# Sums of squares of q and k by two rounded products instead of one full fp32 product

## The chip, the cores and the metric

One core of a Trainium2 chip runs the whole program in one launch. The metric is the device time of that launch in microseconds (us). The engines are named as the profile names them: PE is TensorE, DVE is VectorE, ACT is ScalarE, POOL is GpSimd, SP is SyncE, whose queue issues the DMAs here.

## The reference

A first block (a gated linear recurrence beside windowed attention) and then two layers of a second block work on 256 tokens of width 2048. The change touches the two layers. There, attention normalises q and k by the mean of their squares over each head of 64, and the delta-rule branch normalises q and k of six heads of 128 by the sum of their squares:

```python
qa = apply_partial_rope(rms_norm_2(qa.reshape(bsz, T, A_Q_HEADS, A_HEAD_DIM), q_norm_w[l]), cos, sin)
ka = apply_partial_rope(rms_norm_2(ka.reshape(bsz, T, A_KV_HEADS, A_HEAD_DIM), k_norm_w[l]), cos, sin)
...
def l2_norm(x):
    return x * lax.rsqrt(jnp.sum(x * x, axis=-1, keepdims=True) + EPS)
...
q = l2_norm(q.reshape(bsz, T, C_HEADS, C_HEAD_DIM))
k = l2_norm(k.reshape(bsz, T, C_HEADS, C_HEAD_DIM))
```

## The kernel before

Activations are kept transposed: a tile has 128 features on the partitions and 256 tokens in the free dimension. The large products read their weights in slots of 1 MB (128x2048). A slot is loaded by SP into `w_raw`, rounded by ACT to the type fp32r into `w_hi` (`Ring.round`, L274), and DVE takes the rest `w_raw - w_hi` into `w_lo` (`Ring.residual`, L282). PE then sums three products of rounded operands (hi by hi, hi by lo, lo by hi) for each row of weights. A slot of features is 48 products of 256 columns (`Ring.features`, L309). The ring has five places, so a load starts when the slot five before it is used up; rounding and rest are done some two to three slots ahead of PE.

A layer has 68 slots. Four kinds of slot matter here:

- slots 8 to 11 make k and v of the attention, slots 12 to 17 its q, two slots for each pair of tiles;
- slots 24 to 41 make q, k and v of the six heads of the delta rule, three slots a head;
- slots 42 to 51 make gates, with the chain of the delta rule placed between their products;
- slots 52 to 67 are the output product.

All order is written out by hand. Each engine has one list of instructions for the layer (`sync`, `scalar`, `vector`, `tensor`, `gpsimd` in `layer_parts`), carried out in that order, and the lists are tied by counting semaphores.

The sums of squares over the partitions are products with a matrix of ones on PE. For the attention, ACT squares a pair of tiles into `q_sq` (128x512, L1700 and L1734) and PE multiplies it by `blocks`, ones within each half of 64 (L2582 for k, L2604 for q in `turn_queries`, in the middle of slots 15, 17 and 19). For head h of the delta rule, ACT squares q and k into `sq` (128x512, L1819, at the end of `silu_qk`) and PE multiplies by `ones` (L2652 in `sum_squares`), in the middle of the slot two after the head's last one, or, for the last head, after slot 43. These operands are full fp32, so each of these products stands as two instructions in the trace. A layer has 10 such sums: one for k, three for q, six for the heads.

During the heads' slots the lists of DVE and ACT are tied to each other. For iteration h, DVE's list is: `norm(h - 2)`, `open_heads(h - 1)` (y_now, L2231), the rest of a slot, the convolution of v of the head before (L2241, three taps), `normalise(h)` (L2222), the convolution of q, the rest of a slot, the convolution of k, `soften(h + 1)` (L2197 and on), the rest of a slot. Between them stand pieces of a convolution of 31 taps (L2086, called taps here), of which the last six instructions stand in iteration 3. ACT's list is: a slot's rounding, the evacuation of v (`head_in`), `round_a` (L1786, waits for y_now), `exps`, a slot's rounding, `silu_qk(h - 1)` with the square, `head_in(h, 0)` (L1799, for which DVE's convolution of q waits), and so on. PE waits for the last taps with the first sum of the branch (L2656, after slot 34) and for `normalise` with `flip` (L2635).

POOL does little in a layer: it clears two buffers, prepares masks, takes rests of the attention's output (`split_a`, L2953, one a head), weighs decays (L2967) and takes the rests of the other branch (`branch_split`, L2957).

Of the kernel before, what the change touches and what calls it, by code (L numbers as in the profile page):

```python
# [9 lines left out]
F32 = mybir.dt.float32  # L10
# [378 lines left out]
def first_parts(k, t, s):  # L389
# [933 lines left out]
    "ylo "  # L1323
    "rounded12 split12 bg zcopied rows_in negexp gexped gchain sums scalars scexps "
    "copied conv silued squared summed std norm "
    "bsummed centred bsquared bsquares bstd bln lsig hid bmixed bsteps byrounded bylo "
    "rows grown prepared masked decays weighted ended gout "
# [40 lines left out]
    "ylo": 6, "weighted": 6, "bylo": 4, "stored": 0,  # L1368
}


# [40 lines left out]
def layer_parts(k, t, s, layer):  # L1412
# [23 lines left out]
    assert goto(units_at) <= units_at, "kept parts"  # L1436
    before_decay, until_decay = put("before_decay", [P, 2, H, CHUNK]), put("until_decay", [P, 2, H, CHUNK])
    grown = [put(f"grown{g}", [P, 4, P]) for g in range(G)]
    state_a, vnew = put("state_a", [P, H, P]), put("vnew", [P, G, P])
    o_first = put("o_first", [P, G, P])  # L1440
    second_at = goto(units_at)

    q_raw = [put(f"q_raw{n}", [P, 2, T]) for n in range(2)]
    q_sq, rstd, part = put("q_sq", [P, 2, T]), put("rstd", [P, 2, T]), put("part", [P, 2, T])
    turn = put("turn", [P, P])
    v_rest = put("v_rest", [P, KT - 2 * V_ROWS, V_STEP])
# [49 lines left out]
    padded = put("padded", [P, 3, PAD + T])  # L1496
    goto(k.y_at + 26 * 4 * T)
    conv, sq = put("conv", [P, 3, T]), put("sq", [P, 2, T])
    goto(k.feat_at)
    qk = put("qk", [P, 2 * H, T])  # L1500
    std, bstd = put("std", [P, 2, T]), put("bstd", [P, T])
# [105 lines left out]
    def sync(sp):  # L1607
        ring.load(sp, 3)
        ring.load(sp, 4)
        if layer == 0:  # L1610
            sp.wait_ge(k.first.oroot, 1)
            sp.wait_ge(k.first.ow, 8)
        sp.dma_start(params[:], k.p2[layer]).then_inc(s.p2_in, 16)
        if layer == 0:
            sp.wait_ge(s.joined, since.joined + 10)
            for m in range(2):
                sp.dma_start(t["state"][:, m], x_in[:, m]).then_inc(k.kept, 16)
        ring.load(sp, 5)
        sp.dma_start(sink_row[:], t["sinks_2"][layer:layer + 1].to_broadcast([P, HEADS_2])).then_inc(s.tables_in, 16)
        ring.load(sp, 6)  # L1620
        sp.dma_start(mask[:], constant(k, "window_2")).then_inc(s.tables_in, 16)
        sp.dma_start(cumulate[:], constant(k, "cumulate")).then_inc(s.tables_in, 16)
        sp.dma_start(before[:], constant(k, "before")).then_inc(s.tables_in, 16)
        sp.dma_start(not_before[:], constant(k, "not_before")).then_inc(s.tables_in, 16)
        ring.load(sp, 7)
        sp.dma_start(levels[:].rearrange("p l t -> p (l t)"), constant(k, "levels")).then_inc(s.tables_in, 16)
        sp.dma_start(level_t[:], constant(k, "level_t")).then_inc(s.tables_in, 16)
        sp.dma_start(ident_c[:], constant(k, "ident_c")).then_inc(s.tables_in, 16)
        sp.dma_start(pw[:].rearrange("p a n -> p (a n)"), k.pw[layer]).then_inc(s.tables_in, 16)
        there, arrived = (t["state"], k.kept) if more else (t["out"], s.stored)  # L1630
        for n in range(8, SLOTS_2 + AHEAD):
            ring.load(sp, n)
            if n == 12:
                sp.wait_ge(s.used, since.used + 8)
                sp.dma_start(turn[:], constant(k, "turn_2")).then_inc(s.narrow_in, 16)
                sp.dma_start(v_rest[:].rearrange("p k n -> p (k n)"), k.v_rest[layer]).then_inc(s.narrow_in, 16)
                sp.dma_start(rows[:].rearrange("p a n -> p (a n)"), k.rows_c[layer:layer + 1].to_broadcast([P, 2 * H]))\
                  .then_inc(s.rows_in, 16)
            if n == SLOT_OUT2 + 4:
                sp.wait_ge(s.used, since.used + SLOT_OUT2)  # L1640
                sp.wait_ge(s.bylo, since.bylo + B)
                sp.wait_ge(k.kept, kept_before)
                sp.dma_start(x_t[:], t["state"]).then_inc(s.xin, 16)
            if n == SLOT_OUT2 + 4 and more:

                sp.dma_start(k.norm_w[:], t["p2"][layer + 1, :, P2_NORM:P2_NORM + KT]).then_inc(s.weight_in, 16)
            if n in (SLOT_OUT2 + 11, SLOT_OUT2 + 13, SLOT_OUT2 + 17):
                c = (SLOT_OUT2 + 11, SLOT_OUT2 + 13, SLOT_OUT2 + 17).index(n)
                for m in range(2):
                    sp.wait_ge(s.added, since.added + 2 * c + m + 1)  # L1650
                    sp.dma_start(there[:, m, cols(c)], x_t[:, m, cols(c)]).then_inc(arrived, 16)
        for m in range(2):
            sp.wait_ge(s.added, since.added + 7 + m)
            sp.dma_start(there[:, m, cols(3)], x_t[:, m, cols(3)]).then_inc(arrived, 16)
        if more:
            sp.wait_ge(s.weight_in, since.weight_in + 16)

    def scalar(act):
# [52 lines left out]
        act.activation(v_rest_hi[:], v_rest[:], ACT.Copy).then_inc(s.rounded12, 1)  # L1711
        key_in(1)
        ring.round(act, SLOT_KV + 6)
        act.wait_ge(s.kturned, since.kturned + 2)
        root(aux[3], rstd[:], s.krstd, since.krstd)
        ring.round(act, SLOT_Q + 3)
        act.wait_ge(s.bg, since.bg + 1)
        for b in range(2):
            act.activation(z12[:, b, 0::2], z[b][:, T:V_COLS:2], ACT.Copy).then_inc(s.zcopied, 1)
# [81 lines left out]
        def silu_qk(h):  # L1801
            if h == 0:
                act.wait_ge(k.kept, kept_before)
            act.wait_ge(s.conv, since.conv + 9 * h + 6)
            if h % 2:
                for e in range(2):
                    for i in range(2):
                        ins = act.activation(swapped(qk[:, 2 * h + i], 1 - e), swapped(conv[:, i], e), ACT.Silu)
                    ins.then_inc(s.silued, 1)
            else:  # L1810
                act.activation(qk[:, 2 * h:2 * h + 2], conv[:, 0:2], ACT.Silu).then_inc(s.silued, 1)
            act.wait_ge(s.conv, since.conv + 9 * h + 9)
            if h % 2:
                for e in range(2):
                    act.activation(swapped(v_all[:, h], 1 - e), swapped(conv[:, 2], e), ACT.Silu).then_inc(s.silued, 1)
            else:
                act.activation(v_all[:, h:h + 1], conv[:, 2:3], ACT.Silu).then_inc(s.silued, 1)
            act.wait_ge(s.silued, since.silued + silus_before(h) + 1 + h % 2)
            act.activation(sq[:], qk[:, 2 * h:2 * h + 2], ACT.Square).then_inc(s.squared, 1)  # L1819

        def root_qk(h):
            act.wait_ge(s.summed, since.summed + h + 1)
# [711 lines left out]
    def tensor(pe):  # L2534
# [28 lines left out]
        for j in range(B):  # L2563
# [4 lines left out]
            if j == 0:  # L2568
                pe.wait_ge(s.whole, since.whole + wholes)
                spread_root(pe, k, s, since, KT - 4 * first_c)  # L2570

        pe.wait_ge(s.opened, since.opened + 3)
        for b in range(2):
            ring.features(pe, SLOT_KV + b, tile(2 + b), k.xn_hi, k.xn_lo, None if b else normed_rows)
# [4 lines left out]
        pe.wait_ge(s.kcopied, since.kcopied + 2)  # L2579
        pe.wait_ge(s.emptied, since.emptied + 2)  # L2580
        pe.matmul(aux[2][:, 0:2 * T], turn[:], q_raw[1][:], start=True, stop=True).then_inc(s.kturned, 1)
        pe.matmul(aux[3][:, 0:2 * T], k.blocks[:], q_sq[:], start=True, stop=True).then_inc(s.kturned, 1)  # L2582
        ring.values_and_gates(pe, SLOT_KV + 3, 1, with_gates, k.xn_hi, k.xn_lo)
        pe.wait_ge(s.split12, since.split12 + 1)
        for kk in range(KT - 2 * V_ROWS):
            row = 2 * V_ROWS + kk
# [6 lines left out]
        def turn_queries(i):  # L2593
# [7 lines left out]
                pe.wait_ge(s.rstd, since.rstd + 2)  # L2601
            at = 2 * (i % 2)
            pe.matmul(aux[at][:, 0:2 * T], turn[:], q_raw[i % 2][:], start=True, stop=True).then_inc(s.qturned, 1)
            pe.matmul(aux[at + 1][:, 0:2 * T], k.blocks[:], q_sq[:], start=True, stop=True).then_inc(s.qturned, 1)  # L2604

        def cumulated():
            pe.wait_ge(s.tables_in, since.tables_in + 144)
# [40 lines left out]
            ins.then_inc(mixed[p], 1)  # L2648

        def sum_squares(h):  # L2650
            pe.wait_ge(s.squared, since.squared + h + 1)
            pe.matmul(z[3][:, 0:2 * T], k.ones[:], sq[:], start=True, stop=True).then_inc(s.summed, 1)  # L2652

        def branch_sum(what):
            for b in range(B):
# [254 lines left out]
        for i, (c, w) in enumerate(OUT_ORDER):  # L2910
# [6 lines left out]
                    pe.wait_ge(s.added, since.added + 2 * (c - 1))  # L2917
            if c == 0 and w:
                if w == 1:
                    pe.wait_ge(s.bylo, since.bylo + B)  # L2920
                else:
                    pe.wait_ge(s.olo, since.olo + 1 if w == 2 else G)
            if i < 15:
# [8 lines left out]
    def gpsimd(pool):  # L2932
# [6 lines left out]
        pool.wait_ge(k.kept, 2 * 16)  # L2939
        pool.wait_ge(s.rowed, since.rowed + 1)  # L2940
        pool.memset(padded[:], 0.0).then_inc(s.cleared, 1)
        pool.wait_ge(s.tables_in, since.tables_in + 144)
        pool.wait_ge(s.scalars, since.scalars + 1)
        for r in range(2):
# [9 lines left out]

        def branch_split(b):
            pool.wait_ge(s.byrounded, since.byrounded + b + 1)
            pool.tensor_tensor(k.y_lo[:, 6 + b], yb_now[:, (b + 2) % B], k.y_hi[:, 6 + b].bitcast(F32), ALU.subtract).then_inc(s.bylo, 1)  # L2957

        for u in range(4):
            split_a(u)  # L2960
        for g in range(G):
            if g < 2:
                split_a(4 + g)
            pool.wait_ge(s.decays, since.decays + 2 * g + 1)
            for r in range(2):
                there = before_decay[:, r, 2 * g:2 * g + 2]
# [197 lines left out]
```

## Time and profile before

| what | value |
| --- | --- |
| median of 3 runs | 1921.54 us (1921.5 to 1923.63) |
| time of the profiled execution | 1921.74 us |
| its span, first to last instruction | 1920.0 us |
| granted TensorE clock over the span | 0.998 |
| PE busy | 1900.8 us (99%) |
| DVE busy | 1276.0 us (66%) |
| ACT busy | 1104.2 us (58%) |
| POOL busy | 70.5 us (4%) |
| DMA | 171 GB/s mean |

The time is the span and 1.74 us around it. Busy time of PE counts overlapping matmuls once; the duration of one matmul in the rows (0.28 us for 256 columns) is its passage through the array, and the next one starts before it ends, so a product's cost is read from the distance between starts.

### The profile page before, as it was taken

The numbers are of one execution on the slowest core, as the hardware profiler recorded it, in microseconds if no ns is written. First come the engines' busy times: TensorE is split into PE (matmuls) and PEld (weight loads), VectorE is DVE, ScalarE is ACT, GpSimd is POOL, SyncE is SP. The second block draws the span as 40 slices with busy tenths as digits, with TensorE's granted clock in tenths as the row PEclk, the third lists the DMA queues.
The fourth block names the chain that finished last, engine by engine and source line by source line (L and its number), as shares of the span: only waits on it lengthen the run. The fifth ranks groups of instructions, "written<-read, shape, count | busy, mean of one in ns | idle before, by whom it ended". The sixth has DMA issues, their size and how long they took to land.

```text
span 1920.0 us, 31625 instructions
## 1 busy us (share of the span) xinstructions
PE 1900.8 (99%) x13516; PEld 1703.3 (89%) x13516; DVE 1276.0 (66%) x1791; ACT 1104.2 (58%) x1506; POOL 70.5 (4%) x66
## 2 busy tenths in 40 slices
PE   9999999999999999999999999999999999999998
PEld 8999988888888888888899999998889999999887
DVE  7778766655544444655699898754658988876453
ACT  7787755554533333434656688926465577893541
POOL 0111100000000000000000000100000000010000
PEclk9999999999999999999999999999999999999999
DMA  7454454444455555565564443322666544432163
GB/s 265 181 185 183 160 189 169 154 154 163 164 197 194 188 191 198 191 247 197 188 230 154 176 141 146 132 76 98 225 215 223 176 156 157 150 129 93 67 229 122
DMA packets 52268, 328.92 MB, mean 171 GB/s; under 512 B 7968, under 2 KB 9888, under 8 KB 14368
## 3 DMA queue, kind: packets, MB, share of 16 engines
q1 hardware_dynamic: 52128, 326.90, 47.3%
q8 instruction: 107, 1.75, 0.4%
q14 instruction: 33, 0.27, 0.0%
HBM read 320.59 MB, written 6.29 MB: 170 GB/s over the span
## 4 chain that ended last, share of the span: by engine, by line
PE 96%; ACT 1%; DVE 1%; issue 0%; DMA 0%; SPq 0%; DVEq 0%; ACTq 0%
PE z L309 39%; PE z L333 38%; PE z L320 3%; PE z L321 2%; PE aux L1140 1%; PE aux L2763 1%; PE z L357 1%; PE z L345 1%; PE aux L2665 1%; PE aux L1188 1%; PE aux L1205 1%; PE aux L2768 1%; PE aux L2627 1%; PE z L2652 1%; PE aux L2847 0%
## 5 line engine op out<-in xcount | busy, mean ns | idle before, releaser
L282 DVE TENSOR_TENSOR w_lo<-w_raw,w_hi 128x2048 fp32r<-128x2048 f32 x274 | 631.7, 2308 | 364.3 <-ACT w_hi L274 363.9
L274 ACT ACTIVATE w_hi<-w_raw 128x2048 fp32r<-128x2048 f32 x286 | 546.3, 1915 | 409.4 <-DMA w_raw<-in_w_dram 409.4
L309 PE MATMUL z<-xn,w_hi 128*128 128x256 f32 x3712 | 692.7, 288 | 0.0
L309 PEld LDWEIGHTS z<-xn,w_hi 128*128 128x128 f32 x3712 | 578.8, 191 | 20.1 <-issue 16.8
L309 PE MATMUL z<-xn,w_lo 128*128 128x256 f32 x1856 | 524.7, 283 | 0.0
L333 PE MATMUL z<-w_hi,xn 128*128 128x512 f32 x1136 | 355.5, 391 | 0.0
L309 PEld LDWEIGHTS z<-xn,w_lo 128*128 128x128 f32 x1856 | 355.3, 191 | 0.0
L333 PEld LDWEIGHTS z<-w_hi,xn 128*128 128x128 f32 x1136 | 213.3, 188 | 44.2
L333 PE MATMUL z<-w_lo,xn 128*128 128x512 f32 x568 | 221.0, 389 | 0.0
L333 PE MATMUL z<-w_hi,y_hi 128*128 128x512 f32 x368 | 143.6, 390 | 0.0
L333 PE MATMUL z<-w_hi,y_lo 128*128 128x512 f32 x368 | 143.3, 389 | 0.0
L333 PE MATMUL z<-w_lo,y_hi 128*128 128x512 f32 x368 | 143.2, 389 | 0.0
L333 PEld LDWEIGHTS z<-w_lo,xn 128*128 128x128 f32 x568 | 106.7, 188 | 21.6
L2086 DVE SCALAR_TENSOR_TENSOR acc<-padded_b,params,acc 128x256 f32<-128x256 f32 x240 | 98.5, 478 | 0.0
L320 PE MATMUL z<-xn,w_hi 128*128 128x512 f32 x256 | 92.1, 402 | 0.0
L333 PEld LDWEIGHTS z<-w_hi,y_lo 128*128 128x128 f32 x368 | 69.1, 188 | 14.4
L333 PEld LDWEIGHTS z<-w_hi,y_hi 128*128 128x128 f32 x368 | 69.1, 188 | 14.2
L333 PEld LDWEIGHTS z<-w_lo,y_hi 128*128 128x128 f32 x368 | 69.1, 188 | 14.0
L2241 DVE SCALAR_TENSOR_TENSOR conv<-padded,params,conv 128x256 f32<-128x256 f32 x108 | 58.2, 539 | 31.0 <-ACT conv L1799 28.4
L309 PE MATMUL z<-raw_hi,w_hi 128*128 128x256 f32 x256 | 74.8, 292 | 0.1
L309 PE MATMUL z<-raw_hi,w_lo 128*128 128x256 f32 x256 | 73.1, 285 | 0.0
L309 PE MATMUL z<-raw_lo,w_hi 128*128 128x256 f32 x256 | 73.1, 285 | 0.0
(426 smaller groups left out, 2443.7 us busy)
## 6 DMA issues: line engine op xcount, KB each, us to landing
w_raw<-in_w_dram SPq DMA_DIRECT2D x287, 1024.0 KB, 4.8
gate_w<-in_lru_w_dram SPq DMA_DIRECT2D x8, 512.0 KB, 3.5
x_t<-state_dram SPq DMA_DIRECT2D x2, 2048.0 KB, 9.2
x_first<-in_x_dram SPq DMA_DIRECT2D x4, 512.0 KB, 6.4
x_t<-in_x_dram SPq DMA_DIRECT2D x1, 2048.0 KB, 12.6
state_dram<-x_t SPq DMA_DIRECT2D x2, 1024.0 KB, 5.0
pw<-in_pw_dram SPq DMA_DIRECT2D x2, 1024.0 KB, 6.5
state_dram<-x_t SPq DMA_DIRECT2D x8, 256.0 KB, 6.0
```

The lines of the kernel that those rows point to most:

```text
L274: act.activation(self.k.w_hi[:, self.place(n)], self.k.w_raw[:, self.place(n)], ACT.Copy).then_inc(self.s.rounded, 1)
L282: dve.tensor_tensor(self.k.w_lo[:, at], self.k.w_raw[:, at], self.k.w_hi[:, at].bitcast(F32), ALU.subtract)\
L309: ins = pe.matmul(out, w[:, kk], x[:, kk], start=kk == 0 and j == 0, stop=kk == KT - 1 and j == 2)
L320: pe.matmul(bank[:, 0:2 * T].rearrange("p (b t) -> p b t", b=2), w_hi[:, kk], x[:, :, kk], start=kk == 0, stop=False)
L321: ins = pe.matmul(bank[:, 0:T], w_lo[:, kk], x[:, 0, kk], start=False, stop=kk == KT - 1)
L333: ins = pe.matmul(outs[m], x[:, row, t], w[:, kk], start=row == 0 and j == 0, stop=row == KT - 1 and j == 2)
L345: ins = pe.matmul(outs[m], x[:, row, t], w[:, kk], start=False, stop=row == KT - 1 and j == 2)
L357: ins = pe.matmul(outs[m], x[:, row, t], w[:, kk, 0:V_COLS], start=row == 0 and j == 0, stop=False)
L1140: ins = pe.matmul(aux[2 * b + d][:, g * T:g * T + T], gate_w[i % 2][:, b, 2 * d + g], u_all[:, 2 * i + b], start=True, stop=True)
L1188: ins = pe.matmul(aux[2 * p + h][:, b * T:b * T + T], q_turned[:, 2 * p + h, P * b:P * b + P], keys[:, c], start=True, stop=True)
L2086: dve.scalar_tensor_tensor(out=acc[:, b], in0=padded_b[:, b, n:n + T], scalar=col(w), in1=acc[:, b], op0=ALU.mult, op1=ALU.add).then_inc(s ...
L2241: dve.scalar_tensor_tensor(out=conv[:, i], in0=padded[:, i, tap:tap + T], scalar=col(w), in1=conv[:, i], op0=ALU.mult, op1=ALU.add).then_i ...
```

## The change

The 20 sums (10 in each of the two layers) become two products of fp32r operands each, one with the rounded part of the square and one with the rest, into the same bank (`part_sums`). The matrices of ones are copied once a layer to fp32r. Who makes the two parts:

- For the attention, ACT squares into `q_sq` as before; POOL copies it rounded into `qs_hi` and subtracts, in place of `q_sq`, into `qs_lo` (`part_squares`, two instructions of 128x512 for each of 4 pairs).
- For the heads, ACT's square goes rounded into `sq_hi`; POOL multiplies q and k by themselves into `sq` and subtracts `sq_hi` from it (`part_head`, two instructions of 128x512 for each of 6 heads, after `split_a` of that head).

PE waits for POOL's counter `parted` ahead of each sum. The sum for k moves behind the slot that followed it, and on ACT the rounding of slot 15 moves ahead of k's root. The rest of the diff is places in memory and a counter that two users now share (`ylo` for `bylo`).

```diff
@@ scalar
         ring.round(act, SLOT_KV + 6)
+        ring.round(act, SLOT_Q + 3)
         act.wait_ge(s.kturned, since.kturned + 2)
         root(aux[3], rstd[:], s.krstd, since.krstd)
-        ring.round(act, SLOT_Q + 3)
...
-            act.activation(sq[:], qk[:, 2 * h:2 * h + 2], ACT.Square).then_inc(s.squared, 1)
+            act.activation(sq_hi[:], qk[:, 2 * h:2 * h + 2], ACT.Square).then_inc(s.squared, 1)
@@ tensor
+        def part_sums(bank, weights, hi, lo):
+            pe.matmul(bank[:, 0:2 * T], weights[:], hi[:], start=True, stop=False)
+            return pe.matmul(bank[:, 0:2 * T], weights[:], lo[:], start=False, stop=True)
...
-        pe.matmul(aux[3][:, 0:2 * T], k.blocks[:], q_sq[:], start=True, stop=True).then_inc(s.kturned, 1)
         ring.values_and_gates(pe, SLOT_KV + 3, 1, with_gates, k.xn_hi, k.xn_lo)
+        pe.wait_ge(s.parted, since.parted + 4)
+        part_sums(aux[3], blocks_r, qs_hi, qs_lo).then_inc(s.kturned, 1)
...
-            pe.matmul(aux[at + 1][:, 0:2 * T], k.blocks[:], q_sq[:], start=True, stop=True).then_inc(s.qturned, 1)
+            pe.wait_ge(s.parted, since.parted + 2 * i + 6)
+            part_sums(aux[at + 1], blocks_r, qs_hi, qs_lo).then_inc(s.qturned, 1)
...
-            pe.wait_ge(s.squared, since.squared + h + 1)
-            pe.matmul(z[3][:, 0:2 * T], k.ones[:], sq[:], start=True, stop=True).then_inc(s.summed, 1)
+            pe.wait_ge(s.parted, since.parted + 10 + 2 * h + 2)
+            part_sums(z[3], ones_r, sq_hi, sq_lo).then_inc(s.summed, 1)
@@ gpsimd
+        pool.tensor_copy(ones_r[:], k.ones[:]).then_inc(s.parted, 1)
+        pool.tensor_copy(blocks_r[:], k.blocks[:]).then_inc(s.parted, 1)
+
+        def part_squares(i):
+            pool.wait_ge(s.emptied, since.emptied + (2 * i + 4 if i else 2))
+            if i:
+                pool.wait_ge(s.kturned, since.kturned + 2)
+                after(pool, s.qturned, since.qturned + 2 * i - 2)
+            pool.tensor_copy(qs_hi[:], q_sq[:]).then_inc(s.parted, 1)
+            pool.wait_ge(s.parted, since.parted + 2 + 2 * i + 1)
+            pool.tensor_tensor(qs_lo[:], q_sq[:], qs_hi[:].bitcast(F32), ALU.subtract).then_inc(s.parted, 1)
+
+        for i in range(4):
+            part_squares(i)
+
+        def part_head(h):
+            pool.wait_ge(s.squared, since.squared + h + 1)
+            if h:
+                pool.wait_ge(s.summed, since.summed + h)
+            here = qk[:, 2 * h:2 * h + 2]
+            pool.tensor_tensor(sq[:], here, here, ALU.mult).then_inc(s.parted, 1)
+            pool.wait_ge(s.parted, since.parted + 10 + 2 * h + 1)
+            pool.tensor_tensor(sq_lo[:], sq[:], sq_hi[:].bitcast(F32), ALU.subtract).then_inc(s.parted, 1)
...
         for u in range(4):
             split_a(u)
+            part_head(u)
         for g in range(G):
             if g < 2:
                 split_a(4 + g)
+                part_head(4 + g)
```

## Rows read from the trace of the kernel before

**Rows 1.** The page, part 1: busy us, share, instructions of each engine.

```profile
PE 1900.8 (99%) x13516; PEld 1703.3 (89%) x13516; DVE 1276.0 (66%) x1791; ACT 1104.2 (58%) x1506; POOL 70.5 (4%) x66
```

**Rows 2.** Timeline of PE in slot 15: start, duration, instruction, out<-in.

```profile
1031.38 1.02 PE L2603 MATMUL aux<-q_raw,turn 128*128 128x512 f32 x2
1032.24 1.02 PE L2604 MATMUL aux<-q_sq,blocks 128*128 128x512 f32 x2
```

**Rows 3.** Timeline of PE, first and last of 15 rounded products of 512 columns.

```profile
819.67 0.39 PE L333 MATMUL z<-w_hi,yb_lo 128*128 128x512 f32 x1
...
822.84 0.39 PE L333 MATMUL z<-w_lo,yb_hi 128*128 128x512 f32 x1
```

**Rows 4.** POOL's two-input instructions by line: ns min/median/max, first and last start.

```profile
L525 POOL TENSOR_TENSOR gate_i<-gate_i,u_all x16: 1290/1300/1307, 47.7 to 236.3; 128x512 f32<-128x512 f32 x16
...
L2957 POOL TENSOR_TENSOR y_lo<-yb_now,y_hi x8: 731/889/1110, 1251.6 to 1758.4; 128x256 fp32r<-128x256 f32 x8
```

**Rows 5.** Timeline of DVE, ACT and POOL, heads 0 and 1.

```profile
1117.48 1.52 DVE L2241 SCALAR_TENSOR_TENSOR conv<-padded,params,conv 128x256 f32<-128x256 f32 x3 [2.38 <-ACT conv L1799]
...
1131.72 0.42 ACT L1786 ACTIVATE y_hi<-y_now 128x256 fp32r<-128x256 f32 x1 [2.58 <-DVE y_now L2231]
...
1132.22 2.26 POOL L2953 TENSOR_TENSOR y_lo<-y_now,y_hi 128x256 fp32r<-128x256 f32 x1 [19.77 <-ACT y_hi L1786]
...
1131.60 2.29 DVE L282 TENSOR_TENSOR w_lo<-w_raw,w_hi 128x2048 fp32r<-128x2048 f32 x1
1133.80 2.00 DVE L2241 SCALAR_TENSOR_TENSOR conv<-padded,params,conv 128x256 f32<-128x256 f32 x3
```

**Rows 6.** Waits, 1098 to 1250 us: us in total, times, longest.

```profile
DVE conv L2241 <- ACT conv L1799: 13.9, 6, 6.3
ACT y_hi L1786 <- DVE y_now L2231: 11.3, 4, 3.5
...
PEld z L2656 <- DVE acc L2086: 0.3, 1, 0.3
```

**Rows 7.** Timeline of ACT, DVE and PE, heads 0 to 3 of the first layer.

```profile
1116.13 0.61 ACT L1819 ACTIVATE sq<-qk 128x512 f32<-128x512 f32 x1
...
1161.44 0.62 ACT L1819 ACTIVATE sq<-qk 128x512 f32<-128x512 f32 x1
...
1159.62 1.01 DVE L2222 TENSOR_SCALAR S<-S,small 128x128 f32<-128x128 f32 x4
1160.54 2.46 DVE L2086 SCALAR_TENSOR_TENSOR acc<-padded_b,params,acc 128x256 f32<-128x256 f32 x6
...
1161.67 0.27 PE L2635 MATMUL aux<-ident,S 128*128 128x128 f32 x1
...
1163.28 1.99 PE L2656 MATMUL z<-acc,ones 128*128 128x256 f32 x8
```

**Rows 8.** Timeline of ACT, PE and DVE, heads 3 to 5 of the first layer.

```profile
1185.55 0.61 ACT L1819 ACTIVATE sq<-qk 128x512 f32<-128x512 f32 x1
...
1189.80 1.02 PE L2652 MATMUL z<-sq,ones 128*128 128x512 f32 x2
...
1206.18 0.61 ACT L1819 ACTIVATE sq<-qk 128x512 f32<-128x512 f32 x1
...
1210.44 1.02 PE L2652 MATMUL z<-sq,ones 128*128 128x512 f32 x2
...
1212.97 1.53 DVE L2241 SCALAR_TENSOR_TENSOR conv<-padded,params,conv 128x256 f32<-128x256 f32 x3 [1.72 <-ACT conv L1799]
```

**Rows 9.** Timeline of DVE and PE, head 3 of the second layer.

```profile
1649.00 2.46 DVE L2086 SCALAR_TENSOR_TENSOR acc<-padded_b,params,acc 128x256 f32<-128x256 f32 x6
...
1652.12 1.99 PE L2656 MATMUL z<-acc,ones 128*128 128x256 f32 x8
```

**Rows 10.** Timeline of ACT, the second square of the first pair of q.

```profile
1024.82 0.38 ACT L1734 ACTIVATE q_sq<-z 128x256 f32<-128x256 f32 x1
```

More of the change, by code:

```diff
@@ L1325 @@
     "copied conv silued squared summed std norm "
-    "bsummed centred bsquared bsquares bstd bln lsig hid bmixed bsteps byrounded bylo "
+    "bsummed centred bsquared bsquares bstd bln lsig hid bmixed bsteps byrounded parted "
     "rows grown prepared masked decays weighted ended gout "
@@ L1367 @@
     "ww0": 1, "kv": 3, "so": 4, "ws": 3, "uu1": 1, "ww1": 1, "oturned": 4, "out_half": 1, "cleared": 2, "prepared": 4,
-    "ylo": 6, "weighted": 6, "bylo": 4, "stored": 0,
+    "ylo": 10, "weighted": 6, "parted": 22, "stored": 0,
 }
@@ L1438, in layer_parts @@
     grown = [put(f"grown{g}", [P, 4, P]) for g in range(G)]
+    state_at = goto(0)
+    goto(state_at)
+    sq_hi = put("sq_hi", [P, 2, T], F32R)
+    goto(state_at)
     state_a, vnew = put("state_a", [P, H, P]), put("vnew", [P, G, P])
@@ L1443, in layer_parts @@
     q_raw = [put(f"q_raw{n}", [P, 2, T]) for n in range(2)]
+    square_at = goto(0)
+    goto(square_at)
+    qs_lo = put("qs_lo", [P, 2, T], F32R)
+    goto(square_at)
     q_sq, rstd, part = put("q_sq", [P, 2, T]), put("rstd", [P, 2, T]), put("part", [P, 2, T])
@@ L1498, in layer_parts @@
     conv, sq = put("conv", [P, 3, T]), put("sq", [P, 2, T])
+    goto(k.y_at + 29 * 4 * T)
+    sq_lo = put("sq_lo", [P, 2, T], F32R)
+    ones_r, blocks_r = put("ones_r", [P, P], F32R), put("blocks_r", [P, P], F32R)
+    goto(k.y_at + 12 * 4 * T)
+    qs_hi = put("qs_hi", [P, 2, T], F32R)
     goto(k.feat_at)
@@ L1640, in sync @@
                 sp.wait_ge(s.used, since.used + SLOT_OUT2)
-                sp.wait_ge(s.bylo, since.bylo + B)
+                sp.wait_ge(s.ylo, since.ylo + 6 + B)
                 sp.wait_ge(k.kept, kept_before)
@@ L2919, in tensor @@
                 if w == 1:
-                    pe.wait_ge(s.bylo, since.bylo + B)
+                    pe.wait_ge(s.ylo, since.ylo + 6 + B)
                 else:
@@ L2956, in branch_split @@
             pool.wait_ge(s.byrounded, since.byrounded + b + 1)
-            pool.tensor_tensor(k.y_lo[:, 6 + b], yb_now[:, (b + 2) % B], k.y_hi[:, 6 + b].bitcast(F32), ALU.subtract).then_inc(s.bylo, 1)
+            pool.tensor_tensor(k.y_lo[:, 6 + b], yb_now[:, (b + 2) % B], k.y_hi[:, 6 + b].bitcast(F32), ALU.subtract).then_inc(s.ylo, 1)
         for u in range(4):
             split_a(u)
+            part_head(u)
         for g in range(G):
```

## The prediction

> **What bounds the kernel now.** I read the page's first part: PE is busy 99% of the span and the others far less [rows 1], so PE's own work sets the time and a product taken from PE should shorten it. That holds only as long as PE finds its operands ready, so I then read the list of waits in the stage of the heads and the timeline of DVE, ACT and POOL there. PE waits for almost nothing, but two engines wait for each other: in all six heads DVE's convolution waits for ACT's evacuation, and in four heads ACT waits for DVE's y_now [rows 6]. So from y_now to y_now there is one closed chain: ACT (exps, rounding, silu, square, evacuation), then DVE (convolutions, rests, taps, soften) back to y_now, with next to no slack inside a head. It is not tied to PE, only a little ahead of it. Two places show how little: the last six taps end at 1160.54 + 2.46 = 1163.00 us and PE's branch sum that needs them starts at 1163.28; DVE's normalise ends at 1160.63 and PE's flip, which needs it, starts at 1161.67 [rows 7]. In the second layer the taps end at 1651.46 for 1652.12 [rows 9]. So PE is first, and the chain of ACT and DVE is a close second. What is late by a microsecond on DVE before 1163 us makes PE wait.
>
> **What PE saves.** Two fp32 products that follow each other in slot 15 (two instructions each, 1.02 us in all) start 1032.24 - 1031.38 = 0.86 us apart [rows 2]: one costs 0.86. Fifteen rounded products of 512 columns, each with its own weights, follow each other in (822.84 - 819.67) / 14 = 0.226 us [rows 3]. A sum goes from 0.86 to 0.45: 0.41 less, and 20 of them are 8.1 us: per layer 4 x 0.41 = 1.64 in the attention's part and 6 x 0.41 = 2.46 in the heads'.
>
> **What POOL takes.** An instruction of POOL with two inputs of 512 takes 1.30 us (median of 16), one of 256 at least 0.73 [rows 4]. I take 1.30 for each of a head's two. The copy in the attention's part has no row; one input is no more than two, so it lies between nothing and 1.30. A head's pair, from the end of ACT's square until PE may go, is 0.08 (from ACT's rounding, 1131.72 + 0.42, to POOL's rest at 1132.22 [rows 5]) + 1.30 + an estimated 0.35 for a tap of DVE that gets in between + 1.30 = 3.0 us. PE's sum starts 1189.80 - 1186.16 = 3.64 us after the end of the square of head 3 and 1210.44 - 1206.79 = 3.65 after that of head 4 [rows 8]; these two are the least of the six. Taken alone, POOL is in time everywhere.
>
> **What POOL takes from DVE.** This is the term that decides. POOL's rest of 256 starts at 1132.22, while DVE does a rest of a slot (1131.60 to 1133.89), and takes 2.26 us instead of 0.73: it waits for DVE. DVE's next three taps then take 2.00 us where undisturbed ones take 1.52: DVE waits 0.48 for POOL [rows 5]. So an instruction of POOL and a two-input instruction of DVE exclude each other, the waiting one gets in at the next boundary, and DVE was held for 0.48 of POOL's 0.73, that is for all but 0.25. For 512 columns I take 1.30 - 0.25 = 1.05. Now place a pair: head 0's square ends at 1116.74 [rows 7], POOL multiplies from 1116.82 to 1118.12, and the first tap of DVE's convolution, just released by ACT, wants to start at 1117.48 [rows 5]. It waits until some 0.12 (half of the 0.25) before POOL's end: 0.5. The subtraction gets in behind this tap and holds the second for 1.05. A pair costs the chain 1.55 us. Bounds: 0.96 if each holds DVE only for the 0.48 seen with 256; 2.6 if both are wholly in its way. I take 1.55, by the length of the instruction.
>
> The Trainium skill (SBUF — State Buffer, "Who interferes with whom") says that DVE and GpSimd take a shared pair of ports in turn, for a whole instruction, when DVE has two inputs in SBUF and GpSimd reads it too. By its whole instruction a pair would be 0.64 + 1.30 = 1.9, and the time by the sum below some 1932; the row's 0.48 of 0.73 is shorter, and I go by the row.
>
> **The sum for a layer,** against before, with PE earlier by what its sums saved. Heads 0 and 1 make DVE late by 3.1. PE reaches flip at 1161.67 - 0.82 = 1160.85 and finds normalise ending at 1160.63 + 3.1 = 1163.7: the first wait, 2.9. Head 2's square ends at 1162.06 + 3.1 = 1165.2, while the taps run (now 1163.6 to 1166.1), so both of its instructions hold a tap up: 2 x 1.05 = 2.1 more. The taps end at 1163.0 + 5.2 = 1168.2; PE's branch sum starts there, 4.9 later than before, having waited 5.7 in all with flip. DVE and ACT go on 5.2 late. Sums 2 and 3 bring PE to 4.9 - 0.82 = 4.1 late; head 3's pair is ready at 1186.16 + 5.2 + 3.0 = 1194.4 for 1189.80 + 4.5 = 1194.3, no wait to speak of, but adds 1.55 to the chain. Head 4's square then ends at 1206.79 + 5.2 + 1.55 = 1213.5 and its parts are there at 1216.5; PE arrives at 1210.44 + 4.1 = 1214.5 and waits 2.0. Head 4's pair falls into an idle 1.72 of DVE [rows 8], and ahead of sum 5 POOL has far more than its 3.0. With sums 4 and 5 saved, the heads end 4.1 + 2.0 - 0.82 = 5.3 late. The attention's 1.64 are kept: 5.3 - 1.64 = +3.7 for the first layer; the second has 0.66 instead of 0.28 ahead of its branch sum: +3.3. The profiled execution of 1921.74 (its span and 1.74 around it) becomes 1928.7; the median of before is 0.2 lower: **1928.5 us**.
>
> **Costed at nothing.** For q, the first pair's second square ends at 1025.20 [rows 10] and PE's sum was at 1032.24 [rows 2]: 7.0 us for POOL's two and one rest of a slot of 2.29 in its way (4.9 to 5.2); where a second rest gets in too, 0.2 to 0.5 would be lost a pair. DVE's lateness there (up to 2.3 a pair) ends in its waits for ACT and the weights before the heads begin; without these it would go into the chain as one pair more, 1.55. The sum for k is one slot later and ACT's rounding of slot 15 goes ahead of its root: DVE, queued with its own rest of slot 15 and three steps of the rotation, needs that root only behind them. No DMA is moved; `bylo` and `ylo` are only counted together.
>
> **The rivals.**
>
> - *The saving is all there is.* POOL's pairs fall where DVE doesn't need what they share, and POOL is in time: 1921.74 - 8.1 = 1913.6, as a median 1913.4. For it: PE's 99%, DVE's 66%, the margins of 3.6 for a pair's 3.0. Against: the 0.48 in every head from an instruction half as long, and a square that ends just ahead of DVE's convolution. It decides by the price of a pair p: the lateness at the branch sum is about 3.3 p, and a layer breaks even near p = 0.7; below that the kernel is faster. Chance 0.17.
> - *DVE keeps its turn.* DVE's taps and its rest of a slot get in ahead of POOL's subtraction: a pair then takes 1.0 + 2.28 more and PE waits in the sums of heads 3 and 4 themselves, some 3 us more a layer: 1935. Against: POOL got in between a rest and a tap that was ready [rows 5]. Chance 0.10.
> - *The products aren't cheaper,* because weights loaded behind a wait stand bare: no 8.1, 1937. Against: 0.226 with a load for each [rows 3]. Chance 0.03.
> - *The chain as worked out.* 0.63, with the bounds of p: at 0.96 and shorter instructions of POOL (0.73) the branch sum is 2.9 late, head 4 waits next to nothing, and a layer ends 0.5 to 0.1 ahead of before: 1921; at 2.6 some 1937. Other mishaps: 0.07.
>
> **How the numbers follow.** The likeliest alone has 1921 to 1937. For 8 in 10 I reach a little below, into what lies between it and the first rival (a price of some 0.5 a pair): 1916 to 1937. What a measurement of this kernel can tell from no change is 0.2%, 3.8 us: 1917.7 to 1925.4. Slower: 0.55 of the chain, 0.10 of DVE's turn, 0.03 of the bare weights, 0.03 of the rest, 0.71. Faster: 0.17 and 0.01, 0.18. Same: the rest, 0.11, from the low end of p.
>
> **What would show it.** PE's sums as two products 0.23 apart; waits of PE at flip of head 3, at the branch sum and at the sum of head 4, in place of none; DVE's first two taps behind each square at 0.9 to 1.5 us each instead of 0.5; POOL's two at 1.3 us; slots 12 to 23 shorter by 1.6 us. Wrong I would be if the taps keep their 1.52 behind the squares (no sharing), if DVE has idle time left ahead of y_now in each head, or if POOL's subtraction comes in only behind a rest of a slot.

## The result and the profile after

The change made the kernel slower by 2.8 us: 1924.41 us (median of 22 runs, 1923.82 to 1926.01) against 1921.64 (22 runs, 1920.99 to 1923.63), a ratio of 1.0014 (95% interval 1.0008 to 1.0020). That is less than the 0.2% that the prediction took as telling from no change; with so many runs the interval leaves 1 out. The forecast was 1928.5, so the sign is right and the forecast loss (7.0 us) is 2.5 times the measured one. The profiled execution took 1924.39 us, with a span of 1922.6 for the 1920.0 of before.

The page of the changed kernel, part 1 (busy us, share, instructions) and the head of part 4, the chain that ended last, with the same line of the kernel before below it:

```profile
PE 1895.4 (99%) x13516; PEld 1703.7 (89%) x13516; DVE 1299.7 (68%) x1791; ACT 1103.9 (57%) x1506; POOL 137.7 (7%) x110
...
PE 83%; DVE 8%; ACT 6%; issue 2%; DMA 1%; POOL 0%; SPq 0%; DVEq 0%; ACTq 0%
```

```profile
PE 96%; ACT 1%; DVE 1%; issue 0%; DMA 0%; SPq 0%; DVEq 0%; ACTq 0%
```

PE lost 5.4 us of busy time [rows 1] and DVE gained 23.7: the same 1791 instructions of DVE, held up more often. POOL has 44 instructions more, and still shows 0% in the chain, while DVE and ACT have 14% of it for 2% before. POOL does not set the time by its own work. Where PE now stands is in its list of waits (us in total, times, longest), here the lines that before had not:

```profile
PE aux L2654 <- DVE S L2235: 3.3, 2, 1.9
...
PE z L2586 <- POOL sq_lo L2984: 2.4, 2, 1.2
...
PE z L2586 <- DVE acc L2266: 1.9, 2, 1.0
...
PE z L2675 <- DVE acc L2099: 1.3, 2, 0.6
```

These are one wait of each kind in each layer: at flip of head 3, at the sum of head 4, at the sum of head 2 (whose bank DVE's centring of the branch has to read first), and at the branch sum. They make 8.9 us. The timeline of PE in the first layer shows where they lie:

```profile
1161.12 0.33 PE L2654 MATMUL aux<-ident,S 128*128 128x128 f32 x1 [1.89 <-DVE S L2235]
...
1163.49 1.99 PE L2675 MATMUL z<-acc,ones 128*128 128x256 f32 x8 [0.64 <-DVE acc L2099]
...
1170.03 0.50 PE L2586 MATMUL z<-sq_hi,ones_r 128*128 128x512 f32 x1 [0.96 <-DVE acc L2266]
1170.36 0.39 PE L2587 MATMUL z<-sq_lo,ones_r 128*128 128x512 f32 x1
...
1190.89 0.47 PE L2586 MATMUL z<-sq_hi,ones_r 128*128 128x512 f32 x1
...
1212.58 0.47 PE L2586 MATMUL z<-sq_hi,ones_r 128*128 128x512 f32 x1 [1.22 <-POOL sq_lo L2984]
```

Set against the starts of before [rows 7, 8] (three of them, marked, are from the same timeline and not shown):

| PE starts, first layer | before | after | difference |
| --- | --- | --- | --- |
| sum of head 0 | 1123.01 (not shown) | 1121.21 | -1.80 |
| flip of head 3 | 1161.67 | 1161.12 | -0.55 |
| branch sum | 1163.28 | 1163.49 | +0.21 |
| sum of head 2 | 1168.70 (not shown) | 1170.03 | +1.33 |
| sum of head 3 | 1189.80 | 1190.89 | +1.09 |
| sum of head 4 | 1210.44 | 1212.58 | +2.14 |
| sum of head 5 | 1235.19 (not shown) | 1237.03 | +1.84 |

The attention's part gives what was forecast: 1.64 was worked out, and of the 1.80 at the sum of head 0, 0.21 stood there already ahead of the first changed sum (1003.76 for 1003.97, not shown), so the four sums gave 1.59. The heads give it back and more: PE leaves the last sum 1.84 - 0.40 = 1.44 us late. From -0.21 to +1.44 the first layer costs 1.65 us. The second costs less: at its last sum PE is 3.04 late (1727.07 for 1724.03, not shown) and leaves it 2.64 late, 1.2 more than at the end of the first. The spans differ by that 2.6, the medians by 2.8.

The ledger for the whole run: 20 sums save 8.1; four kinds of wait cost 8.9; what is left, 2.8 + 8.1 - 8.9 = 2.0 us, lies for the most part as 0.1 to 0.25 us at each of the stops and of the sums behind them, where the first product after a wait starts without one ahead of it (0.33 us for flip's first against the 0.27 of [rows 7]). That last part is read from the differences and was not tried by itself.

On the side of DVE and POOL, at head 0, where the chain gets late for the first time (timelines of DVE and POOL, changed kernel, first layer):

```profile
1115.71 2.62 DVE L2254 SCALAR_TENSOR_TENSOR conv<-padded,params,conv 128x256 f32<-128x256 f32 x3 [2.37 <-ACT conv L1812]
...
1115.05 1.04 POOL L2982 TENSOR_TENSOR sq<-qk 128x512 f32<-128x512 f32 x1 [4.36 <-ACT sq_hi L1832]
1116.17 1.36 POOL L2984 TENSOR_TENSOR sq_lo<-sq,sq_hi 128x512 fp32r<-128x512 f32 x1
```

The three taps took 2.62 us for 1.52 [rows 5]: **one pair costs the chain 1.10 us**, with the same idle 2.37 ahead of it. In narrow windows the same timeline shows the taps one by one:

```profile
1115.71 0.66 DVE L2254 SCALAR_TENSOR_TENSOR conv<-padded,params,conv 128x256 f32<-128x256 f32 x1 [2.37 <-ACT conv L1812]
1116.41 1.41 DVE L2254 SCALAR_TENSOR_TENSOR conv<-padded,params,conv 128x256 f32<-128x256 f32 x1
1117.85 0.48 DVE L2254 SCALAR_TENSOR_TENSOR conv<-padded,params,conv 128x256 f32<-128x256 f32 x1
```

Beside the third, which meets no instruction of POOL, the first is 0.18 longer (it starts 0.66 after POOL's product) and the second 0.93 (it meets the subtraction). And around head 2, whose square ends among the last six taps of the branch:

```profile
1160.98 2.46 DVE L2099 SCALAR_TENSOR_TENSOR acc<-padded_b,params,acc 128x256 f32<-128x256 f32 x6
1163.35 3.09 DVE L2254 SCALAR_TENSOR_TENSOR conv<-padded,params,conv 128x256 f32<-128x256 f32 x3
1166.37 2.28 DVE L282 TENSOR_TENSOR w_lo<-w_raw,w_hi 128x2048 fp32r<-128x2048 f32 x1
1168.57 1.40 DVE L2266 SCALAR_TENSOR_TENSOR acc<-z,acc 128x256 f32<-128x256 f32 x4
...
1162.56 2.17 POOL L2982 TENSOR_TENSOR sq<-qk 128x512 f32<-128x512 f32 x1 [4.15 <-ACT sq_hi L1832]
1164.81 1.35 POOL L2984 TENSOR_TENSOR sq_lo<-sq,sq_hi 128x512 fp32r<-128x512 f32 x1
```

The six taps take their old 2.46. POOL's product, at 1162.56 in the middle of them, takes 2.17 for the 1.04 of head 0 and ends 1.3 us after the taps do. The convolution behind the taps takes 3.09 for 1.52. So the pair does not hold up the taps, for which PE waits next; it holds up what follows, and then the centring that PE needs in the sum of head 2.

### The profile page after: what moved, and what is told of

Read it like the earlier page. It is cut to its first block, busy times and chain, and to the rows that moved or that the text cites. A ratio compares the mean times of both kernels' runs of the same rounds, so it can differ in the third digit from the quotient of the medians.

```text
span 1922.6 us, 31685 instructions
## 1 busy us (share of the span) xinstructions
PE 1895.4 (99%) x13516; PEld 1703.7 (89%) x13516; DVE 1299.7 (68%) x1791; ACT 1103.9 (57%) x1506; POOL 137.7 (7%) x110
## 4 chain that ended last, share of the span: by engine, by line
PE 83%; DVE 8%; ACT 6%; issue 2%; DMA 1%; POOL 0%; SPq 0%; DVEq 0%; ACTq 0%
PE z L333 38%; PE z L309 29%; PE z L320 3%; DVE w_lo L282 2%; DVE conv L2254 2%; PE z L321 2%; PE aux L1140 1%; PE aux L2782 1%; ACT w_hi L274 1%; PE z L357 1%; DVE acc L2099 1%; PE z L345 1%; ACT S L1785 1%; PE aux L2684 1%; PE aux L1205 1%
## 5 line engine op out<-in xcount | busy, mean ns | idle before, releaser
L274 ACT ACTIVATE w_hi<-w_raw 128x2048 fp32r<-128x2048 f32 x286 | 546.4, 1915 | 410.3 <-DMA w_raw<-in_w_dram 410.2
L309 PE MATMUL z<-xn,w_hi 128*128 128x256 f32 x3712 | 685.4, 286 | 0.0
L2099 DVE SCALAR_TENSOR_TENSOR acc<-padded_b,params,acc 128x256 f32<-128x256 f32 x240 | 104.1, 500 | 0.0
L2254 DVE SCALAR_TENSOR_TENSOR conv<-padded,params,conv 128x256 f32<-128x256 f32 x108 | 69.9, 647 | 27.9 <-ACT conv L1812 25.2
```

The source lines that it names most:

```text
L274: act.activation(self.k.w_hi[:, self.place(n)], self.k.w_raw[:, self.place(n)], ACT.Copy).then_inc(self.s.rounded, 1)
L309: ins = pe.matmul(out, w[:, kk], x[:, kk], start=kk == 0 and j == 0, stop=kk == KT - 1 and j == 2)
L2099: dve.scalar_tensor_tensor(out=acc[:, b], in0=padded_b[:, b, n:n + T], scalar=col(w), in1=acc[:, b], op0=ALU.mult, op1=ALU.add).then_inc(s ...
L2254: dve.scalar_tensor_tensor(out=conv[:, i], in0=padded[:, i, tap:tap + T], scalar=col(w), in1=conv[:, i], op0=ALU.mult, op1=ALU.add).then_i ...
```

## The experiments

The theory to be tried: the products save what was worked out, and POOL's pairs take it back by holding up DVE in the heads, not by being late themselves. Rivals: the products save less (their weights stand bare behind a wait); POOL is late itself; or any work on POOL or any new wait of the lists is enough. All times are medians of the kernel against 1921.6 to 1921.8 of before.

**The attention's part alone.** In the changed kernel the heads go back to one fp32 product.

```diff
+SPLIT_HEADS = ()
-            act.activation(sq_hi[:], qk[:, 2 * h:2 * h + 2], ACT.Square).then_inc(s.squared, 1)
+            act.activation((sq_hi if h in SPLIT_HEADS else sq)[:], qk[:, 2 * h:2 * h + 2], ACT.Square).then_inc(s.squared, 1)
...
+            if h in SPLIT_HEADS:
...
+            else:
+                pe.wait_ge(s.squared, since.squared + h + 1)
+                pe.matmul(z[3][:, 0:2 * T], k.ones[:], sq[:], start=True, stop=True).then_inc(s.summed, 1)
```

> Only the sums of the attention (k and q, 4 a layer) are split; the heads are as before. Theory (POOL's pairs cost only where DVE has no slack, in the heads): 8 x 0.41 = 3.3 us are gained in full, 1918.3 for a before of 1921.6. Rival (the pairs cost DVE as much ahead of the heads): little or nothing gained, 1920 to 1922.

Measured: 1918.86 us, ratio 0.9986 (0.9977 to 0.9994).

**The heads' part alone.** The other half: `part_squares` goes, the four sums of the attention are fp32 again, and k's sum and ACT's rounding of slot 15 are back where they were.

> Only the sums of the heads (6 a layer) are split. Theory: the whole loss sits here, 1924.4 + 3.3 = 1927.7, with PE's waits at flip of head 3, the branch sum, and the sums of heads 2 and 4 as in the changed kernel. Rival (the loss is spread over both parts): 1922 to 1926.

Measured: 1927.29 us, ratio 1.0029 (1.0018 to 1.0039). The halves are -2.7 and +5.7; together +3.0, and the change has +2.8. They add up within 0.2 us, and the loss is the heads' alone.

**The pair without the products.** To the kernel before, POOL's two instructions of each head are added, into a place that nothing reads; the sums stay fp32.

```diff
+        def part_head(h):
+            pool.wait_ge(s.squared, since.squared + h + 1)
+            here = qk[:, 2 * h:2 * h + 2]
+            pool.tensor_tensor(sq_x[:], here, here, ALU.mult).then_inc(s.parted, 1)
+            pool.wait_ge(s.parted, since.parted + 2 * h + 1)
+            pool.tensor_tensor(sq_x[:], sq_x[:], sq[:], ALU.subtract).then_inc(s.parted, 1)
```

> The kernel before, with its full fp32 sums, and POOL's pair of each head beside them, into a place that nobody reads. PE gains nothing and never waits for POOL. Theory (the pairs hold up DVE, and PE is held to the chain of ACT and DVE): the chain is late by two pairs of 1.1 and by 1.6 in the third, less a margin of 0.7 at the sum of head 2, so PE is 3.1 us late a layer, and 1927 to 1928 for before 1921.6; DVE's three taps behind a square take 2.6 us instead of 1.5. Rival (PE's waits for POOL's result make the loss): 1921.6, no change.

Measured: 1928.30 us, ratio 1.0034 (1.0021 to 1.0048). Its timeline of DVE at head 0, and its waits of PE that are not before's:

```profile
1117.06 2.62 DVE L2249 SCALAR_TENSOR_TENSOR conv<-padded,params,conv 128x256 f32<-128x256 f32 x3 [2.37 <-ACT conv L1804]
```

```profile
PE z L2660 <- DVE acc L2261: 1.9, 2, 1.0
...
PE z L2664 <- DVE acc L2094: 1.3, 2, 0.6
PE aux L2643 <- DVE S L2230: 1.3, 2, 0.7
```

The same 2.62, and waits for DVE at the same three places, though PE waits for nothing that POOL makes. (ACT does wait for POOL's counter here, ahead of the next square and of the root, so that no place is overwritten; ACT's list of waits shows no wait for POOL.) Flip's is shorter (0.7 for 1.9), because here PE has saved nothing and comes later. The pair by itself costs 6.7 us.

**POOL busy, but only writing.** The same as above with two memsets of 1280 columns in place of the pair.

> As the run with the pair beside the old sums, but POOL's two instructions only write (two memsets of 1280 columns, some 1.2 us each by the 1.05 for 1144). Theory (what is shared is the reading of SBUF): no change, 1921.6, DVE's taps 1.5 us. Rival (any instruction of POOL holds DVE up, or the additional semaphores do): as with the pair, 1927.

Measured: 1921.72 us, ratio 1.0001 (0.9992 to 1.0010). Timelines of POOL and DVE at head 0:

```profile
1117.65 1.17 POOL L2968 MEMSET sq_wide<- 128x1280 f32 x1 [4.35 <-ACT sq L1825]
1118.88 1.17 POOL L2970 MEMSET sq_wide<- 128x1280 f32 x1
```

```profile
1118.33 1.52 DVE L2247 SCALAR_TENSOR_TENSOR conv<-padded,params,conv 128x256 f32<-128x256 f32 x3 [2.37 <-ACT conv L1803]
```

2.34 us of POOL across DVE's three taps, and these keep 1.52. So it is neither POOL being busy nor the new counter (ACT's wait ahead of the next square is kept in this run; the one ahead of the root is not). What separates this from the pair, besides the operation, is that the pair reads its operands from memory and a memset reads nothing. The Trainium skill (SBUF — State Buffer, "Who interferes with whom") says so: a DVE instruction with two inputs in SBUF contends with a GpSimd one that reads SBUF, and not with one that only writes. The two runs agree with it, 2.62 against 1.52.

**The products without the pair.** The changed kernel, with ACT's rounded square used twice against a matrix of halves. It leaves out the rests of the squares, so its sums are those of the rounded parts alone.

```diff
-            return pe.matmul(bank[:, 0:2 * T], weights[:], lo[:], start=False, stop=True)
+            return pe.matmul(bank[:, 0:2 * T], weights[:], hi[:], start=False, stop=True)
...
-            pe.wait_ge(s.parted, since.parted + 10 + 2 * h + 2)
-            part_sums(z[3], ones_r, sq_hi, sq_lo).then_inc(s.summed, 1)
+            pe.wait_ge(s.squared, since.squared + h + 1)
+            hi_sum(z[3], ones_r, sq_hi).then_inc(s.summed, 1)
```

> All 20 sums as two products of rounded operands, but POOL makes no parts: both products take the rounded square, with a matrix of halves, so the rest of the square is left out of the sums; PE waits for ACT's square alone. Theory: PE gains 8.1 less what the chain of ACT and DVE holds it back at the branch sum (it comes 0.82 earlier and had 0.28 and 0.66 to spare: 0.5 and 0.2), 1914.2 for a before of 1921.6. Rival (the rounded products are not cheaper behind a wait, or the heads lose for another reason): 1917 to 1922.

Measured: 1915.06 us, ratio 0.9965 (0.9952 to 0.9977): 6.8 us faster, for 8.1 worked out. Of the missing 1.3, 0.7 is a wait in its list, in both layers together (for the other 0.6 none is listed):

```profile
PE z L2674 <- DVE acc L2099: 0.7, 2, 0.5
```

With PE earlier, the last taps are what it waits for. That is the small margin of 0.28 us that the prediction read in [rows 7], and with it the products give 1915 as the kernel stands, not 1913.4.

**Fewer heads.** The changed kernel with the heads' split for the last head, the last two and the last three (`SPLIT_HEADS` of the first experiment: 5; 4, 5; 3, 4, 5).

> The attention's sums and that of the last head alone are split. Theory: head 5's pair falls behind y_now of head 4 and ahead of nothing that PE waits for: 0.8 better than the attention alone (10 sums of 20): 1917.7 where that gave 1918.5.

> The attention's sums and those of heads 4 and 5 are split (12 of 20). Theory: head 4's pair falls into DVE's idle 1.7 us, and its 2.6 us fit into the 3.65 ahead of PE's sum as long as the chain is not late: 1.6 better than the attention alone, 1916.9. Rival (each pair costs its 1.1 wherever it stands): 1919 to 1921.

> The attention's sums and those of heads 3, 4 and 5 are split (14 of 20). Theory: head 3's pair makes y_now of head 4 late by 1.1, so the parts of head 4 come 0.5 after PE: a gain of 0.41 a layer against a wait of 0.5, no better than heads 4 and 5 alone, 1916.9 to 1917.2.

Measured, with the attention's part alone and the change for comparison:

| heads with two products | us | ratio (interval) |
| --- | --- | --- |
| none | 1918.86 | 0.9986 (0.9977 to 0.9994) |
| 5 | 1917.84 | 0.9981 (0.9972 to 0.9989) |
| 4, 5 | 1916.95 | 0.9975 (0.9966 to 0.9984) |
| 3, 4, 5 | 1917.52 | 0.9978 (0.9969 to 0.9987) |
| all | 1924.41 | 1.0014 (1.0008 to 1.0020) |

Heads 4 and 5 give 0.9 to 1.0 us each, the 0.82 of two sums. With head 3 as well, PE waits for POOL in one layer:

```profile
PE z L2588 <- POOL sq_lo L2992: 0.7, 1, 0.7
```

and the gain ends (the 0.6 us between these two versions is less than their runs scatter). Heads 0 to 2, ahead of the branch sum, cost 6.9 us. The version with heads 4 and 5 beats both kernels, by 4.7 us and 7.5 us.

**Why the pair of head 2 came in behind the taps.** Each of the last six taps waits for the tap two ahead of it (there are two sums in turn), so the next one is ready when one ends. The edit makes them wait for the one directly ahead, which leaves a gap between them. It was put into the changed kernel and into the one before.

```diff
-                    dve.wait_ge(s.taps, since.taps + 2 * at + b - first - 1)
+                    dve.wait_ge(s.taps, since.taps + 2 * at + b - first - (0 if at >= 2 * TAPS_B - 3 else 1))
```

> The change, with the last six taps of the 31-tap convolution made one chain (each waits for the one directly ahead of it, not for the one two ahead). Theory (POOL gets its turn only when DVE's next instruction is not ready at the moment the last one ends): now there is a gap behind every tap, so POOL's product of head 2 starts between the taps and takes 1.0 to 1.5 us in place of 2.17; the six taps take 3.9 to 5 us in place of 2.46; the convolution behind them takes close to 1.5 in place of 3.09; PE waits 1 to 2 us more at the branch sum (1.5 to 2.5 for 0.64) and less at the second sum; time 1924.4 to 1926.5. Rival (POOL has to let DVE finish any such row of instructions, gap or none, or the pair costs the same wherever it lands): POOL's product still takes 2.2 or more and ends just behind the taps, the taps take some 3.0, the same as in the kernel before with the same edit; the convolution behind them stays at 3.1; time 1925 to 1926 from the slower taps alone.

> The kernel before with the same edit (last six taps one chain), as the measure of what the edit costs by itself. Both theories: the six taps take about 3 us in place of 2.46 (each waits for the one ahead to end and signal), PE's branch sum starts 0.3 us later in the first layer and at its old time in the second, time within 0.5 of before, 1921.3 to 1922.3.

Measured: in the kernel before, 1922.20 us, ratio 1.0003 (0.9993 to 1.0012), the six taps at 3.08 us; in the changed kernel 1928.29 us, ratio 1.0033 (1.0021 to 1.0046), with these timelines, the first line from the kernel before with the edit, the others of DVE and POOL in the changed kernel with it:

```profile
1160.12 3.08 DVE L2086 SCALAR_TENSOR_TENSOR acc<-padded_b,params,acc 128x256 f32<-128x256 f32 x6
...
1160.99 4.84 DVE L2099 SCALAR_TENSOR_TENSOR acc<-padded_b,params,acc 128x256 f32<-128x256 f32 x6
1165.74 1.52 DVE L2254 SCALAR_TENSOR_TENSOR conv<-padded,params,conv 128x256 f32<-128x256 f32 x3
...
1162.57 1.04 POOL L2982 TENSOR_TENSOR sq<-qk 128x512 f32<-128x512 f32 x1 [4.16 <-ACT sq_hi L1832]
1163.69 1.33 POOL L2984 TENSOR_TENSOR sq_lo<-sq,sq_hi 128x512 fp32r<-128x512 f32 x1
```

POOL starts at the same 1162.57 and now takes 1.04, both instructions lie among the taps, these take 4.84 for 3.08, and the convolution behind them is back at 1.52. In this row of taps the gap decides who goes first: with none, the six taps kept POOL out until they were over. It is not the whole rule. In [rows 5] POOL's rest got in ahead of the convolution's first tap though no gap is there: the rest of a slot ends at 1133.89 and the tap, whose input ACT had ready at 1129.14 (not shown), is recorded from 1133.80 on and takes 0.96 us for 0.48:

```profile
1133.80 0.96 DVE L2241 SCALAR_TENSOR_TENSOR conv<-padded,params,conv 128x256 f32<-128x256 f32 x1
```

What makes that boundary different from one between two taps was not tried.

PE's waits at the branch sum came out at 1.76 and 3.02 us for the expected 1.5 to 2.5:

```profile
PE z L2675 <- DVE acc L2099: 4.8, 2, 3.0
```

The time was expected at 1924.4 to 1926.5 (the rival's at 1925 to 1926) and is 1.8 above that. The windows of this run show why (PE's granted clock is the number after POOL's count):

```profile
1160.00:1161.00 1.00, 0.00 (x0) 0.00 (x0) 0.96 (x6) 1.00 (x1) 0.00 (x0) 1.00 0.90 164
1161.00:1162.00 1.00, 0.87 (x5) 0.87 (x6) 0.95 (x3) 0.99 (x4) 0.00 (x0) 0.66 0.63 262
1162.00:1163.00 1.00, 1.00 (x7) 0.67 (x7) 0.94 (x2) 1.00 (x3) 0.43 (x1) 0.50 1.10 467
...
1660.00:1662.00 2.00, 2.00 (x6) 1.53 (x6) 2.00 (x2) 0.00 (x0) 0.00 (x0) 0.50 0.00 0
```

The clock fell to 0.50 (the lower of the two levels, 1.2 GHz) behind PE's stop at flip and stayed there for some 10 us (0.61 on the mean from 1170 to 1172). The eight products of the branch sum took 3.78 us for 1.99. From the branch sum to the sum of head 2 PE took 8.10 us, where the changed kernel took 6.54, of which 0.96 were a wait: 2.5 us to the clock. In the second layer the clock is at 0.50 behind the stop of 3.02 us at the branch sum too, and the same stretch takes 7.04 us for 6.54: 1.5 us. Without these 4.0 us the profiled execution of 1928.79 would be at 1924.8, inside what was expected: an estimate from these rows.

## Why the prediction was right in sign and too large

**PE's saving: right.** Two products 1121.21 to 1121.45, 0.24 us apart, for 0.226 worked out. The attention's part alone gave 2.7 of 3.3 in the medians, and 1.59 a layer between the same products in its trace; heads 4 and 5 gave 0.9 to 1.0 for 0.82 each, all 20 without POOL's work 6.8 of 8.1.

**POOL's instructions: one of two.** The subtraction takes 1.34 us on the mean (1.30 forecast); the product of a tile with itself 1.04. The nearest row [rows 4] is a product of two different operands; that the same operand twice takes less was not to be seen in it, and what makes the difference was not tried. The pair is ready 2.5 us after the square, for 3.0.

**The price of a pair, 1.55: the term that was mis-sized.** It is 1.10 us (2.62 against 1.52, the same in the run with the pair alone). Of the forecast's two parts, 0.5 behind the product is 0.18, since the product is over sooner, and 1.05 behind the subtraction is 0.93; of what was to show it, both taps at 0.9 to 1.5 us, only the second came true (0.66 and 1.41). Heads 0 and 1 together make DVE 2.2 late and not 3.1: the taps start at 1160.98, 0.44 later than before [rows 7] in a kernel whose head 0 started 1.77 earlier [rows 5]. Flip waits 1.9 and not 2.9. This term is most of the miss: on the prediction's own scale (a layer breaks even at 0.7 and loses some 3.5 at 1.55) a price of 1.10 loses some 1.65 a layer, 3.3 in all, which is an estimate, for 2.8 measured and 7.0 forecast.

**Head 2: the step that failed.** The prediction let both of its instructions in between the last six taps (2.1 us) and had PE wait for that at the branch sum, 4.9 late without the attention's gain, 3.3 with it. The rows showed the taps untouched, the branch sum only 0.21 late, and 1.57 us at the convolution behind instead. From there a wait came that was not foreseen, for the centring, at the sum of head 2: PE was 1.33 late there and not 3.3. "The waiting one gets in at the next boundary" was drawn from one place [rows 5]; the run with the taps in one chain shows it to hold where each of DVE's instructions waits for the one ahead: there POOL goes in between, for 1.76 us. In the row of ready taps it did not hold. By the estimate above this mistake moved the wait more than it moved the time.

**Head 3 without a wait: right. Head 4: 1.2 us for 2.0**, since the pair is quicker and DVE less late. So the layers lost 1.65 and 1.2 us and not 3.7 and 3.3.

**How much of it was luck.** The range of 1916 to 1937 holds gains as well as losses. What the prediction called no change, 1917.7 to 1925.4, had a chance of 0.11, and 1924.41 lies in it; its sign is sure only because all 22 runs lie above all 22 of before (1923.82 and more, 1923.63 and less). The sign itself, with 0.71 for slower, was argued from the mechanism that the runs bear out.

**The rivals.** "The saving is all there is" falls with the run of the pair alone, +6.7. But its condition was near: with a pair at 1.10 us against the 0.7 at which the prediction let a layer break even, a loss of 2.8 us is what is left of two sums that almost cancel, 8.1 and 10.9. "DVE keeps its turn" was right about one thing, that DVE's ready instructions keep POOL out, and wrong about the place: the wait came in the taps at head 2. Whether it made the loss smaller there, by keeping POOL out of what PE needed next, is not shown: the run that lets POOL in is 3.9 us slower, of which the clock, by the estimate above, takes some 4.0. "The products aren't cheaper" falls with 1915.06.

What stays open: when a waiting POOL gets in ahead of a DVE instruction that is ready (it did behind the rest of a slot, and not between the taps), the 2.0 us of the ledger that lie outside the listed waits, and why the clock fell behind flip's wait of 1.80 in one kernel and not behind one of 1.89 in the other.

## What to carry to other kernels

Work given to POOL is not free because POOL is idle: a pair of two-input instructions that read SBUF, 2.4 us in all, cost DVE's two-input taps 1.10 us at head 0 and 1.76 among the chained taps, and what that is worth is read from the engine that PE waits for next, not from DVE's busy share. Place such work behind the last point where PE is close to DVE's chain (here heads 4 and 5, behind the branch sum): the same edit for 12 of the 20 sums then gains 4.7 us where it lost 2.8. Where two engines exclude each other, look at whether the next instruction of the one is ready when the last one ends: here a row of independent taps kept the other out, and the same row with each tap waiting for the last let it in. Behind the rest of a slot, 2.3 us long, it got in all the same.

## What the runs showed of the hardware that was not expected

- POOL's copy with rounding, one input, is short where it meets little of DVE and long beside DVE's long instructions. In the changed kernel: all eight copies (ns min/median/max, first and last start), then POOL and DVE at a short one and at the longest:

```profile
L2970 POOL CAST qs_hi<-q_sq x8: 973/2624/3448, 1000.5 to 1541.4; 128x512 fp32r<-128x512 f32 x8
...
1038.06 0.98 POOL L2970 CAST qs_hi<-q_sq 128x512 fp32r<-128x512 f32 x1 [9.11 <-ACT q_sq L1747]
...
1000.54 3.45 POOL L2970 CAST qs_hi<-q_sq 128x512 fp32r<-128x512 f32 x1 [41.23 <-ACT q_sq L1713]
...
1000.59 2.28 DVE L282 TENSOR_TENSOR w_lo<-w_raw,w_hi 128x2048 fp32r<-128x2048 f32 x1
```

  The prediction had set the copy between nothing and 1.30, which its shortest ones keep; the median of 2.62 us is not the copy's own length. The parts are there 2.0 us or more before PE's sums, so this cost nothing.
- A product of one tile with itself takes POOL 1.04 us, less than any two-input row of 512 columns before (1.29 to 1.31 [rows 4]). By line, POOL in the changed kernel (busy us, mean ns; the product of head 2 with its 2.17 us is in the mean):

```profile
L2984 POOL TENSOR_TENSOR sq_lo<-sq,sq_hi 128x512 fp32r<-128x512 f32 x12 | 16.1, 1339 | 0.9
L2982 POOL TENSOR_TENSOR sq<-qk 128x512 f32<-128x512 f32 x12 | 14.8, 1229 | 57.8 <-ACT sq_hi L1832 57.8
```

- A memset of 1280 columns (1.17 us) runs beside DVE's two-input taps at no cost to them.
- Six taps of DVE that are always ready kept a waiting POOL instruction out for 1.1 us, and let it in at once when each waited for the one ahead.
- It is not only DVE's instructions with two tiles as inputs that get longer. In the kernel before, four steps of DVE's normalise that scale one tile by a column take 2.49 us beside POOL's products of 384 columns (from 1091.31 to 1093.77), for 1.01 us in [rows 7]:

```profile
1091.62 2.49 DVE L2222 TENSOR_SCALAR S<-S,small 128x128 f32<-128x128 f32 x4
```
